# GpSimd's gate and residual work at the end of each half moves to the vector engine

## What is computed

```python
h = rms_norm(x, norm1_g[l]) * (1.0 + sc1) + sh1
proj = h @ w_in[l]
# attention | conformer convolution | short gated convolution | pooling -> ya, yb, yc, yd
mix = jnp.concatenate([ya, yb, yc, yd], axis=-1) @ w_out[l]
x = x + g1 * mix
h = rms_norm(x, norm2_g[l]) * (1.0 + sc2) + sh2
x = x + g2 * (jnp.square(jax.nn.relu(h @ w_ff1[l])) @ w_ff2[l])
```

## Time and profile before

| | us |
|---|---|
| median of 3 runs | 2347.94 |
| lowest, highest | 2343.76, 2510.97 |
| the profiled execution | 2347.8 |
| its span | 2346.0 |
| PE busy | 2230.1 (95%) |
| DVE busy | 1840.0 (78%) |
| ACT busy | 1121.7 (48%) |
| POOL busy | 404.3 (17%) |

### The profile page before, as it was taken

The page is one execution under the profiler, slowest core; times in us unless marked ns, Lnnn a source line. Parts: engine busy times, 40 slices in busy tenths (PEclk is TensorE's granted clock), DMA queues, the critical chain, the costliest instruction groups (busy, mean ns, idle before and its releaser), DMA issues. The chain is left out here.

```text
span 2346.0 us, 29756 instructions
## 1 busy us (share of the span) xinstructions
PE 2230.1 (95%) x11258; PEld 1875.4 (80%) x11258; DVE 1840.0 (78%) x2575; ACT 1121.7 (48%) x1787; POOL 404.3 (17%) x301
## 2 busy tenths in 40 slices
PE   7999999988999999999998999998999999899997
PEld 5987897767889888788886888877878888688886
DVE  6548796889989876876677888897687777788888
ACT  4531555458988754433334444532443333444441
POOL 0442044824355520000000000030000000000003
PEclk9999999989999989999999999999999999999999
DMA  7441534120000054144446344455244444643434
GB/s 270 152 157 55 166 115 133 62 82 28 15 10 24 10 175 148 68 155 154 159 158 230 119 169 146 159 213 164 91 138 148 153 149 149 223 171 132 165 134 161
DMA packets 168523, 311.54 MB, mean 133 GB/s; under 512 B 10665, under 2 KB 82621, under 8 KB 167357
## 3 DMA queue, kind: packets, MB, share of 16 engines
q1 hardware_dynamic: 168292, 309.60, 38.7%
q10 hardware_dynamic: 88, 0.04, 0.0%
HBM read 219.42 MB, written 90.18 MB: 132 GB/s over the span
## 5 line engine op out<-in xcount | busy, mean ns | idle before, releaser
L1166 POOL TENSOR_TENSOR sb_out<-sb_out,sb_gate_row 128x1024 f32<-128x1024 f32 x8 | 20.5, 2565 | 1433.0 <-DVE sb_out L2343 1433.0
L2878 PE MATMUL ps<-sb_h_hi 128*128 128x512 f32 x512 | 203.6, 398 | 23.1 <-DVE sb_out L2343 13.0
L2879 PE MATMUL ps<-sb_h_lo,sb_h_hi 128*128 128x512 f32 x512 | 202.2, 395 | 0.0
L2880 PE MATMUL ps<-sb_h_hi,sb_h_lo 128*128 128x512 f32 x512 | 202.2, 395 | 0.0
L2844 PE MATMUL ps<-sb_h_hi,sb_w_hi 128*128 128x512 f32 x448 | 178.2, 398 | 17.6 <-DVE sb_u_full L2375 10.6
L2527 PE MATMUL ps<-sb_h_hi,sb_w_hi 128*128 128x512 f32 x448 | 177.8, 397 | 0.7 <-DVE sb_w_lo L2195 0.7
L2845 PE MATMUL ps<-sb_h_lo,sb_w_hi 128*128 128x512 f32 x448 | 177.5, 396 | 0.0
L2529 PE MATMUL ps<-sb_h_hi,sb_w_lo 128*128 128x512 f32 x448 | 174.5, 390 | 0.0
L2528 PE MATMUL ps<-sb_h_lo,sb_w_hi 128*128 128x512 f32 x448 | 174.4, 389 | 0.0
L2076 DVE TENSOR_SCALAR_CACHE_REDUCE sb_scores<-ps 128x1024 f32<-128x1024 f32 (+7 forms) x160 | 139.6, 891 | 15.6 <-PE ps L2741 8.5
L2879 PE MATMUL ps<-sb_w_lo,sb_w_hi 128*128 128x512 f32 x384 | 149.4, 389 | 0.0
(11 more groups left out here) (341 smaller groups left out, 6074.9 us busy)
## 6 DMA issues: line engine op xcount, KB each, us to landing
left_scratch<-sb_u_sum SPq DMA_DIRECT2D x128, 256.0 KB, 6.5
sb_right<-in_w_ff SPq DMA_DIRECT2D x16, 2048.0 KB, 8.6
sb_h_lo_full<-left_scratch SPq DMA_DIRECT2D x64, 512.0 KB, 3.7
sb_w_full<-in_w_ff SPq DMA_DIRECT2D x28, 1024.0 KB, 6.4
left_scratch<-sb_u_full SPq DMA_DIRECT2D x96, 256.0 KB, 2.0
sb_w_full<-left_scratch SPq DMA_DIRECT2D x48, 512.0 KB, 3.3
sb_w_raw<-in_w_in SPq DMA_DIRECT2D x16, 1024.0 KB, 5.7
sb_ada<-in_w_ada SPq DMA_DIRECT2D x32, 512.0 KB, 5.2
```

The costliest lines, as they stand in the source:

```text
L2878: M(dst, hi[:, k, tok], hi[:, 2 + k, :], start=fresh and k == 0, stop=False, skip_group_check=True)
L2879: M(dst, hi[:, k, tok], low[:, 2 + k, :], start=False, stop=False, skip_group_check=True)
L2880: ins = M(dst, low[:, k, tok], hi[:, 2 + k, :], start=False, stop=k == 1, skip_group_check=True)
```

## The change

`finish_upper` on GpSimd is gone, and its sixteen instructions are written into DVE's list, each gate product right behind an evacuation. The gate products and row sums that DVE had already are moved in its list as well: the gate products of `out21` now stand ahead of evacuation (1, 0), the row sums of `out21` between the evacuations (1, 0) and (1, 1), those of `out22` near the end. Row sums of a pair are now one instruction of 128 x 1024 in place of two of 128 x 512 where the rows lie together. In half 0 the last slot's products and the two `wo_tail` with them are moved ahead of `out22`'s. `upper_done` is raised three times per half instead of four, and its waits on SP and ACT are renumbered; the list of SP's instructions is otherwise the same.

```diff
--- before.py
+++ after.py
@@ -880,7 +880,7 @@
 
             def store_out(hc, e):
                 if e < 4:
-                    sp.wait_ge(upper_done, 4 * hc + 3 + e // 2)
+                    sp.wait_ge(upper_done, 3 * hc + 2 + e // 2)
                 else:
                     sp.wait_ge(lower_done, 4 * hc + e - 3)
                 sp.dma_start(out_v[:, hc * HT + e, :], x_late(e)).then_inc(out_st[e // 2], 16)
@@ -992,7 +992,7 @@
                         load_mix(HT + n)
                     sp.wait_ge(part_mm, part_no(G, 3, 3))
                     load_w_out(1, 1)
-                    sp.wait_ge(upper_done, 2)
+                    sp.wait_ge(upper_done, 1)
                     load_w_out(1, 3)
                     sp.wait_ge(part_mm, part_no(G, 5, 3))
                     load_w_out(1, 2)
@@ -1157,20 +1157,6 @@
             pool.wait_ge(o_read, NT)
             pool.tensor_tensor(out=att_sq_last[:, :, :], in0=att_tiles(LAST), in1=att_tiles(LAST),
                                op=ALU.mult).then_inc(asq_ready, 1)
-
-            def finish_upper(hc, s, part, a):
-                col = slice(a * BLK, (a + 1) * BLK)
-                for p in range(2):
-                    y = part[:, 2 * p:2 * p + 2, :]
-                    pool.wait_ge(part_read, read_no(hc, CHUNKS - 1, s, p))
-                    link(pool.tensor_tensor(out=y, in0=y, in1=gate_row[:, 1:2, col].to_broadcast([P, 2, BLK]), op=ALU.mult))
-                    pool.wait_ge(x_late_ld[p], 16 + 32 * (hc + 1))
-                    rows = x_pair[p][:, :, col]
-                    pool.tensor_tensor(out=rows, in0=rows, in1=y, op=ALU.add).then_inc(upper_done, 1)
-
-            for hc in range(2):
-                finish_upper(hc, 1, out11, 0)
-                finish_upper(hc, 3, out12, 1)
 
 
         @block.scalar
@@ -1696,7 +1682,7 @@
                     mix_head(HT)
                     mix_head(HT + 1)
                     wo_head(1, 2, (part_mm, part_no(G, 5, 3)))
-                    wo_head(1, 3, (upper_done, 4))
+                    wo_head(1, 3, (upper_done, 3))
 
 
         @block.vector
@@ -2465,55 +2451,82 @@
                 def gate_of(a, n):
                     return gate_row[:, 1:2, a * BLK:(a + 1) * BLK].to_broadcast([P, n, BLK])
 
-                def scaled(y, a, n):
-
-                    link(V.tensor_tensor(out=y, in0=y, in1=gate_of(a, n), op=ALU.mult))
-
-                def add_to_row(e, a, y):
-                    dve.wait_ge(x_late_ld[e // 2], 16 + 32 * (hc + 1))
-                    row = x_late(e)[:, a * BLK:(a + 1) * BLK]
-                    return V.tensor_tensor(out=row, in0=row, in1=y, op=ALU.add)
+                def scaled(s, p, a):
+
+                    y = sum_of(s, p)
+                    dve.wait_ge(part_read, read_no(hc, c, s, p) if s != 6 else read_no(hc, c - 1, 6, 1))
+                    link(V.tensor_tensor(out=y, in0=y, in1=gate_of(a, 2), op=ALU.mult))
+
+                def add_to_rows(p, a, y):
+
+                    col = slice(a * BLK, (a + 1) * BLK)
+                    if p < 3:
+                        dve.wait_ge(x_late_ld[p], 16 + 32 * (hc + 1))
+                        rows = x_pair[p][:, :, col]
+                        return V.tensor_tensor(out=rows, in0=rows, in1=y, op=ALU.add)
+                    dve.wait_ge(x_late_ld[3], 16 + 32 * (hc + 1))
+                    for i in range(2):
+                        row = x_one[i][:, 0, col]
+                        ins = V.tensor_tensor(out=row, in0=row, in1=y[:, i, :], op=ALU.add)
+                    return ins
+
+                def last_product(t):
+                    dve.wait_ge(part_mm, part_no(chunk_no(hc, c), SLOTS - 1, t))
+                    ins = V.tensor_tensor(out=out21[:, t, :], in0=psum[:, 4 + t, :], in1=gate_row[:, 1, 0:BLK], op=ALU.mult)
+                    if t % 2:
+                        ins.then_inc(part_read, 1)
+
+                def finish_row(t):
+                    dve.wait_ge(part_read, read_no(hc, c, 6, t // 2))
+                    row = x_late(4 + t)[:, 0:BLK]
+                    V.tensor_tensor(out=row, in0=row, in1=out21[:, t, :], op=ALU.add).then_inc(lower_done, 1)
 
                 evacuate(c - 1, 6, 1)
                 tails(c, 5)
                 tails(c, 6)
+                for p in range(2):
+                    scaled(6, p, 0)
                 evacuate(c, 1, 0)
+                for p in range(2):
+                    add_to_rows(2 + p, 0, sum_of(6, p))
                 evacuate(c, 1, 1)
                 for p in range(2):
-                    scaled(sum_of(6, p), 0, 2)
+                    scaled(1, p, 0)
                 evacuate(c, 5, 0)
                 evacuate(c, 5, 1)
                 dve.wait_ge(part_read, read_no(hc, c, 5, 1))
                 for p in range(2):
                     V.tensor_tensor(out=sum_of(3, p), in0=sum_of(3, p), in1=sum_of(5, p), op=ALU.add)
                     link(V.tensor_tensor(out=sum_of(4, p), in0=sum_of(4, p), in1=sum_of(5, p), op=ALU.add))
-                for t in range(4):
-                    add_to_row(4 + t, 0, out21[:, t, :])
+                for p in range(2):
+                    ins = add_to_rows(p, 0, sum_of(1, p))
+                ins.then_inc(upper_done, 1)
                 evacuate(c, 3, 0)
                 evacuate(c, 3, 1)
+                scaled(3, 0, 1)
+                evacuate(c, 4, 0)
+                scaled(3, 1, 1)
+                add_to_rows(0, 1, sum_of(3, 0)).then_inc(upper_done, 1)
+                evacuate(c, 4, 1)
+                add_to_rows(1, 1, sum_of(3, 1)).then_inc(upper_done, 1)
                 if hc == 0:
                     wo_tail(1, 0)
-                for p in range(2):
-                    evacuate(c, 4, p)
-                    dve.wait_ge(part_read, read_no(hc, c, 4, p))
-                    scaled(sum_of(4, p), 1, 2)
-                    for t in (2 * p, 2 * p + 1):
-                        add_to_row(4 + t, 1, out22[:, t, :])
-                if hc == 0:
                     wo_tail(1, 1)
+                    for t in range(4):
+                        last_product(t)
                     mix_tail(HT)
                     mix_tail(HT + 1)
-                for t in range(4):
-                    dve.wait_ge(part_mm, part_no(chunk_no(hc, c), SLOTS - 1, t))
-                    ins = V.tensor_tensor(out=out21[:, t, :], in0=psum[:, 4 + t, :], in1=gate_row[:, 1, 0:BLK], op=ALU.mult)
-                    if t % 2:
-                        ins.then_inc(part_read, 1)
-                        dve.wait_ge(part_read, read_no(hc, c, 6, t // 2))
-                        for r in (t - 1, t):
-                            add_to_row(4 + r, 0, out21[:, r, :]).then_inc(lower_done, 1)
-                if hc == 0:
                     wo_tail(1, 2)
                     wo_tail(1, 3)
+                for p in range(2):
+                    scaled(4, p, 1)
+                    add_to_rows(2 + p, 1, sum_of(4, p))
+                for t in range(4):
+                    if hc:
+                        last_product(t)
+                    if t % 2:
+                        finish_row(t - 1)
+                        finish_row(t)
 
 
         @block.tensor
```

## The result

The changed kernel takes 2358.84 us (median of 5 runs, 2354.58 to 2359.34), the kernel before 2346.75 us in the same comparison. The ratio is 1.0056, 95% interval 1.0041 to 1.0071: slower by some 13 us, clear of noise, and within 2%. It is taken without the one slow run of the kernel before (2510.97 us); the median of its other four is 2345.76 us. Run again beside other kernels it was 2360.5 us against 2344.5 us, ratio 1.0072 (1.0058 to 1.0085).

A forecast was written before the change was run, and what follows sets the result against it. PE was taken to bound the program as a whole, but not its last 26 us, where DVE is busy and its order decides. 2347.8 + 5.0 (half 0) + 10.6 (half 1) = 2363.4 us, range 2352 to 2378.

The forecast's parts named there:

- the start of the sum: The time of the kernel before, to which both halves' losses were added: 2347.8 us, as profiled.
- Evacuation (1, 0) late by two gate products: Ahead of slot 5, two out21 gate products (2.5 us) come first on DVE, so PE waits 2.3 us.
- DVE held by the loads: Between evacuations (1, 0) and (1, 1), DVE idles some 6.5 us, then some 1 us more, for rows 4 to 7.
- PE's stop in slot 5: In half 1, tiles 2 and 3 wait for evacuation (1, 1): PE stands 8.6 us, then runs at a lower clock.
- The stall of slot 6 goes: Late in half 1, PE's old 4.89 us wait for evacuation (4, 1) disappears.
- What follows: After half 1's last row sum, the last stores take an unchanged 4.5 us.
- Half 0: At the end of half 0, the w_out product starts at 1601.3 against 1596.29: 5.0 us later.
- The backlog behind it: Work put off past half 0's w_out start hides in DVE's 4.00 us idle: costed at nothing, 0.6 us if uncovered.
- The engine itself: At each half's end, moving GpSimd's work adds 9.6 us to DVE and returns 9.4 us of stretching.
- the first (no wait): Slot 5: rows are there in time or their wait does not hold PE; 2342.0 us, faster than before; chance 0.08.
- the third (stretching that is not GpSimd's): Ends of halves: transfers or DVE itself stretch DVE's instructions, so moved work costs 8 us more per half, 2379; chance 0.03.
- the clock one: PE's clock stays low through slots 2 to 4 and 6: +14 us per half at most, 2391; chance 0.04.

The follow-up runs named there:

- e2: e1 with the two gate products of out21 also moved ahead of the last slot's operand splits: 2333.97 us, ratio 0.9964.
- e6: The changed kernel with the three out21 row sums adding out21 to itself, so they wait for no load: 2339.4 us, ratio 0.9987.
- e1: The changed kernel with the three out21 row sums for rows 4 to 7 put behind the four sums with part5: 2338.99 us, ratio 0.9978.
- e7: The changed kernel with SP loading rows 4 to 7 first and rows 0 to 3 behind them: 2349.46 us, ratio 1.0033.
- e10: The changed kernel itself run once more for a second trace: 2360.5 us, ratio 1.0072.
- e9: The kernel before with GpSimd's sixteen operations done by DVE, the order of the rest of DVE's list kept: 2343.6 us, ratio 0.9991.
- e3: The kernel before with GpSimd's sixteen operations at the ends of the halves cut to one column in 512: 2329.87 us, ratio 0.9941.
- e5: The changed kernel with e1's edit in half 0 only: 2348.79 us, ratio 1.0027.

## Why the prediction held

2363.4 us was forecast and 2358.84 measured. The loss itself was forecast at 15.6 us; it is 14.9 us in the two stretches and 13 and 17 us by the two ratios. Some 2 us of the gap between the two times lie in the start of the sum: it was 2347.8 us, the profiled execution, and the median beside it (2347.94) had the run of 2510.97 us as one of three. Step by step:

- **Evacuation (1, 0) late by two gate products**, PE 2.3 us: 2.33 us in every trace that has this order, and gone in e2.
- **DVE held by the loads.** Some 6.5 us were forecast for rows 4 and 5 and some 1 us for rows 6 and 7; in half 1 6.60 and 1.29 us came. e6, e1 and e7 take the wait away in three ways (no load needed, another place, a sooner landing), and each time the loss goes with it, in e7 in proportion.
- **PE's stop in slot 5.** 8.6 us forecast, 7.04 us in half 1 and 7.90 us in half 0 (8.61 and 9.54 us in e10). It is shorter where the clock had fallen already and the tiles before it ended later. The restart is set by DVE, so this does not move the end.
- **The stall of slot 6 goes**, the DVE chain behind it is as worked out: the last row sum ends 49.5 us after the splits (50.0 in e10), forecast 49.9. What follows took 3.9 us, not 4.5. This is no effect of the change: the prediction misread a row. The last row sum before starts at 2340.83 and takes 1.29 us, so it ends at 2342.1 and not at 2341.5, and 3.9 us followed it there too. The two terms, 0.4 and 0.6 us, are the 1.0 us by which half 1 was over-priced (10.6 against 9.6).
- **Half 0**: 5.0 forecast, 5.26 and 4.5 measured. The backlog behind it was put at nothing, and at 0.6 us if its cover failed. It did fail: DVE takes the first result of the `w_out` product 62.06 us behind the splits, without a wait, against 56.24 us before. That is +5.8 us, 0.6 more than A (5.0 and 0.6 in e10). PE waits 1.2 us in all ahead of its transposes (0.4 in e10). In the change:

```profile
1607.66 0.68 DVE L2171 TENSOR_TENSOR sb_wo_gated<-ps,sb_gate_row 128x512 f32<-128x512 f32 x1
```

- **The engine itself**: neutral by e9. The prediction had 9.6 us of work for 9.4 of stretching per half. By DVE's busy time in the whole program (1840.0 us before, 1819.3 in e3, 1838.1 in e9) the stretching is 20.7 us and the work 18.8 us, an estimate of 10.4 and 9.4 us per half. The prediction's count left out the gate product of 2.13 us at 2333.61 (in e3's section), 0.9 us over its own time. It was not part of the sum that gave 2363.4. The rivals fall: the first (no wait) by the rows above, the third (stretching that is not GpSimd's) by e3, the clock one by PE's full clock (1.00 granted) from 2320 us on.

**Why the loss is less than the stop.** PE stands 9 to 12 us at slot 5 in each half, where it did not stand before, and A grows by only 5 us. The new order pays this back in slot 6. The prediction reads that PE stood there once per half before; that is so in half 1, but in half 0 PE stood twice, 8.1 us together:

```profile
1579.18 0.47 PE L2878 MATMUL ps<-sb_h_hi 128*128 128x512 f32 x1 [3.63 <-DVE sb_out L2343]
1587.94 0.80 PE L2878 MATMUL ps<-sb_h_hi 128*128 128x512 f32 x1 [4.44 <-DVE sb_out L2343]
```

Both waits are gone in the change. In half 1 the stall in slot 6 is gone too, but DVE's own list sets the end there, so that this gains nothing. From the splits to its last row sum DVE was idle 0.4 us before and is idle 10.7 us now, with 0.8 us less work: the sum comes 9.6 us later.

**A version that beats both**: e2, 0.9964 of the kernel before (0.9951 to 0.9976), some 8 to 9 us less than before and some 22 us less than the change. It is the change with two groups of lines moved: the row sums of `out21` (e1) and its gate products.

## What to carry to other kernels

When work is moved into another engine's list, ask of every instruction what it waits for, and then who needs what stands behind it: three row sums that nobody was in need of, put ahead of one evacuation, held TensorE 7 to 9.5 us in each half. A transfer's wait belongs behind the last instruction that another engine needs before the data can be there; the row of its landing gives that time. Taking elementwise work off GpSimd was free here. A DVE instruction with both inputs in SBUF that began beside a GpSimd one was held until that one's end, and this added up to what the same work costs on DVE (some 10 us per half). Look for such long instances of a form beside short ones.

## What the runs showed of the hardware

After a stop of 2.33 us the clock of PE sometimes fell and sometimes did not, in the same code. In the change's half 1, and below it in e10's:

```profile
2304.29 0.42 PE L2892 MATMUL ps<-sb_h_lo,sb_h_hi 128*128 128x512 f32 x1
2304.52 0.62 PE L2893 MATMUL ps<-sb_h_hi,sb_h_lo 128*128 128x512 f32 x1
2304.94 0.63 PE L2891 MATMUL ps<-sb_h_hi 128*128 128x512 f32 x1
```

```profile
2308.15 0.39 PE L2893 MATMUL ps<-sb_h_hi,sb_h_lo 128*128 128x512 f32 x1
2308.39 0.40 PE L2891 MATMUL ps<-sb_h_hi 128*128 128x512 f32 x1
```

In the first the matmuls are 0.42 us apart from the sixth on, the pace of the lower level (1.2 GHz), in the second 0.23 us, that of 2.4 GHz. Where nothing else waits this shows in the time. e5 and e1 have the same order in half 0; the clock fell in e5 and not in e1, and evacuation (5, 1) started 11.2 us after the splits against 9.7 us, and A is 1.6 us longer. What decides between the two was not tried.
